# Front and middle of a hybrid state-space block: loads, weight buffers, product blocks, row copies and channel norm in another order

## The reference

```python
sh1, sc1, g1, sh2, sc2, g2 = split(silu(cond) @ ada_w + ada_b, 6)
h = rmsnorm(x + pos, norm1_g) * (1 + sc1) + sh1
z = h @ w_in                              # 1280 columns: 512 | 256 | 512
# 512: state-space mixer, 32 groups of 16 channels, 64 complex states, both directions
y = u * d + sum over directions of Re(C @ scan(lam_bar, B_bar @ u))
y = gelu(y); y_ssm = y * sigmoid(y @ w_glu + b_glu)
# 256: pooling, windows 2, 4, 8, 16: (mean - token) @ pool_w * scale
# 512: v = a * sigmoid(g); 31 depthwise taps; layer norm over 256 channels; silu
x = x + g1 * (concat(y_ssm, y_pool, y_conv) @ w_out)
h2 = rmsnorm(x, norm2_g) * (1 + sc2) + sh2
x = x + g2 * ((silu(h2 @ w1) * (h2 @ w3)) @ w2)   # then a last rmsnorm
```

## Time and profile before

| | us |
|---|---|
| three runs | 1328.51, 1330.0, 1331.0; median 1330.0 |
| profiled execution, first to last instruction (span) | 1323.8 |
| PE busy | 1220.8 (92%) |
| DVE, POOL, ACT busy | 850.8, 516.0, 511.0 |
| start of input projection block 0, end of block 29 | 66.8, 299.7 |
| glu tiles begin | 363.06 |

### The profile page before, as it was taken

How to read it: one execution, slowest core, us unless ns; L and a number is a source line. 1 busy time by engine, 2 the same in 40 slices (tenths; PEclk the granted TensorE clock), 3 DMA queues, 4 the chain that set the end, 5 groups by cost and what they waited for, 6 DMA issues and landing times.

```text
span 1323.8 us, 21436 instructions
## 1 busy us (share of the span) xinstructions
PE 1220.8 (92%) x7574; PEld 1080.5 (82%) x7574; DVE 850.8 (64%) x1338; ACT 511.0 (39%) x911; POOL 516.0 (39%) x360
## 2 busy tenths in 40 slices
PE   6786978995599999899999999999999999999996
PEld 4486877895545788799999999999889999999995
DVE  5538539959973427677666667766865555555558
ACT  2652531117235646633333333333532333334223
POOL 0595104376233101654444455444443233333340
PEclk9897988898799999999999999999999999999998
DMA  8815054389791331866665766666768777777771
GB/s 308 339 64 157 28 163 150 105 95 211 204 400 64 128 112 64 270 225 221 206 217 187 246 222 227 217 207 220 260 193 276 246 256 256 260 254 263 244 275 75
DMA packets 189570, 268.52 MB, mean 203 GB/s; under 512 B 14031, under 2 KB 108537, under 8 KB 186825
## 3 DMA queue, kind: packets, MB, share of 16 engines
q1 hardware_dynamic: 188144, 263.07, 60.6%
q0 software_dynamic: 1280, 4.72, 0.9%
q10 hardware_dynamic: 88, 0.02, 0.0%
HBM read 186.49 MB, written 81.26 MB: 202 GB/s over the span
## 4 chain that ended last, share of the span: by engine, by line
PE 76%; DMA 5%; issue 4%; POOL 4%; ACT 4%; DVE 3%; SPq 3%; DVEq 0%; ACTq 0%; POOLq 0%
PE banks L862 22%; PE banks L864 22%; PE banks L863 22%; PE banks L1131 3%; DMA ad<-in_ada_w 1%; PE banks L898 1%; PE banks L947 1%; SPq L436 1%; ACT nts L1660 1%; PE banks L1013 1%; POOL psum_w L751 1%; POOL sst L791 1%; DMA z_dram<-zp 1%; POOL pu L757 1%; PE banks L1136 1%
## 5 line engine op out<-in xcount | busy, mean ns | idle before, releaser
L814 POOL TENSOR_TENSOR raw13r<-raw13s,w13h 128x512 fp32r<-128x512 f32 x110 | 155.1, 1418 | 467.1 <-ACT w13h L1612 421.9
L863 PE MATMUL banks<-ntr,w13h 128*128 128x256 f32 (+1 forms) x1144 | 336.1, 294 | 0.0
L862 PE MATMUL banks<-ntr,w13h 128*128 128x256 f32 (+1 forms) x968 | 282.5, 292 | 4.4 <-ACT xs L1622 2.3
L863 PEld LDWEIGHTS banks<-ntr,w13h 128*128 128x128 f32 x1144 | 215.5, 188 | 0.9
L862 PEld LDWEIGHTS banks<-ntr,w13h 128*128 128x128 f32 x968 | 182.5, 189 | 6.5 <-ACT xs L1622 2.6
L862 PE MATMUL banks<-f2h,f_hi 128*128 128x512 f32 x396 | 156.6, 395 | 0.4 <-DVE acc L2317 0.4
L864 PE MATMUL banks<-f2h,f_lo 128*128 128x512 f32 x396 | 156.2, 395 | 0.0
L863 PE MATMUL banks<-f2l,f_hi 128*128 128x512 f32 x396 | 156.2, 394 | 0.0
L864 PE MATMUL banks<-ntr,raw13r 128*128 128x256 f32 (+1 forms) x528 | 153.5, 291 | 0.0
L2183 DVE TENSOR_TENSOR acc<-acc,banks 128x512 f32<-128x512 f32 x170 | 112.7, 684 | 38.9 <-PE banks L864 30.8
L818 POOL TENSOR_TENSOR f2l<-f2s,f2h 128x1024 fp32r<-128x1024 f32 x44 | 106.1, 2432 | 34.1 <-ACT f2h L1616 34.1
(11 more groups left out here) (323 smaller groups left out, 2536.4 us busy)
## 6 DMA issues: line engine op xcount, KB each, us to landing
raw13s<-in_ffn_w SPq DMA_DIRECT2D x66, 512.0 KB, 4.5
parts<-w13h SPq DMA_DIRECT2D x110, 256.0 KB, 2.4
w13h<-parts SPq DMA_DIRECT2D x110, 256.0 KB, 2.7
f2s<-in_ffn_w SPq DMA_DIRECT2D x44, 512.0 KB, 4.2
ad<-in_ada_w SPq DMA_DIRECT2D x20, 1024.0 KB, 9.8
parts<-wsumr SPq DMA_DIRECT2D x66, 256.0 KB, 2.6
wsumr<-parts SPq DMA_DIRECT2D x55, 256.0 KB, 4.9
parts<-raw13r SPq DMA_DIRECT2D x44, 256.0 KB, 2.9
```

The costliest lines, as they stand in the source:

```text
L814: nc.gpsimd.tensor_tensor(w13_low(x, f), w13_low(x, f, F32), w13h[x][:, :, :].bitcast(F32), ALU.subtract).then_inc(sem("w13_lo"), 1)
L862: nc.tensor.matmul(out, hi_w, hi_x, start=start, stop=False)
L863: nc.tensor.matmul(out, hi_w, lo_x, start=False, stop=False)
```

## The change

Front: on SP the first two `ada` pieces go ahead of `raws` and the position tables, x and columns of `w_in` follow in another order; four loads go to ACT's queue. A third buffer for `w_in` columns, low parts 0 and 1 on POOL and 2 on DVE. PE runs blocks 0 and 1 ahead of most turns, blocks 4 to 8 ahead of the first `wb_turn`, one block between the states' inputs, and in the loop two blocks for each two halves. Reading back `u` is split from writing `z`. DVE adds positions 4 to 7 later.

Middle: `sst` becomes four tiles; POOL copies all of quarter 0 right after the scan and half of each other quarter, ACT the other half between its evacuations of `y`; `u` has four buffers, and 2 and 3 are read between the `wc` quarters. Half of the last `y` writes go on ACT's queue. The gate of the first conv half moves up on POOL; the low parts of the glu product move from DVE to POOL. The channel mean comes after the last glu tile, the second mean after part of the output product.

```diff
-    wst = [at(f"wst{i}", [P, KT, P], O_WS + 4096 * i) for i in range(2)]
+    wst = [at(f"wst{i}", [P, KT, P], a) for i, a in enumerate((O_WS, O_WS + 4096, O_W2))]
-    sst = at("sst", [P, 2, Q, UC], O_NT + 36864)
+    sst = [at(f"sst{e}", [P, 2, 2, 4, UC], O_WB + 9408 if e == 0 else O_NT + 36864 + 9216 * e) for e in range(4)]
-    OUT = (4, 5, 0, 1, 6, 7, 2, 3)
+    OUT = (4, 5, 0, 1, 2, 3, 6, 7)
+    W_SLOT = (0, 1, 2, 0, 1, 0, 1, 0, 1, 0)
+    W_PRIOR = (None, None, None, 0, 1, 3, 4, 5, 6, 7)
+    LOW_POOL = (0, 1, 5, 6, 7, 8, 9)
+    def row_copy(e, r, d, par):
+        return (view(sst[e], (2 * par + d) * 4 * UC, [[UC, 4], [BL, NBL], [1, BL]], NS * r, NS),
+                view(st, r * Q * SLOTS + NPAIR * d + 4 * e, [[1, 4], [Q, NBL], [SLOT, BL]], NS * par, NS))
...
# SP: start
+        ada_in(0)
+        ada_in(1)
         for i, name in enumerate(("ssm_b_re", "ssm_b_im", "ssm_c_re", "ssm_c_im")):
...
-        for n in range(4):
-            x_in(n)
-            ada_in(n)
+        x_in(0)
+        ada_in(2)
+        x_in(1)
+        ada_in(3)
+        x_in(2)
+        x_in(3)
         ada_in(4)
...
+        for i in range(2):
+            z_saved(i)
+            sp.wait_ge(sem("z_out"), 16 * (i + 1))
+            u_first(i)
+        z_saved(2)
+        sp.wait_ge(*low_ready(3))
+        w_in_load(5)
+        z_saved(3)
+        sp.wait_ge(sem("z_out"), 64)
+        for i in range(2, 4):
+            sp.wait_ge(sem("v_done"), 8 * (i - 1))
+            u_first(i)
+        sp.wait_ge(*low_ready(4))
+        w_in_load(6)
...
+            if e in (1, 2):
+                u_again(e + 1)
...
# SP: y
-            if j + 2 < 4:
-                sp.wait_ge(sem("y_done"), 2 * (j + 1))
-                u_again(j + 2)
-            for t in range(CH):
+            for t in range(CH if j < 3 else CH // 2):
...
# POOL
+        w_low(0)
         pool.wait_ge(sem("gsc"), 1)
...
-        for n in range(8):
+        wc_piece(0)
+        w_low(1)
+        for n in range(1, 8):
             wc_piece(n)
+        w_low(5)
...
                     w_low(7 + 2 * j)
+                    if j == 1:
+                        gate_conv(0)
...
+        pool.wait_ge(sem("scan_done"), 1)
+        for r in range(2):
+            for d in range(2):
+                for par in range(2):
+                    nc.gpsimd.tensor_copy(*row_copy(0, r, d, par)).then_inc(sem("st_copied_pool"), 1)
+        pool.wait_ge(sem("st_copied_pool"), 8)
+        gate_conv(1)
...
         for m in range(4):
             glu_out(m)
             wo_low(m + 2)
+            y_low(m, ym[m % 2][:, :], m + 3)
...
# PE
         z_block(0)
-        x_turns(10, 13)
         z_block(1)
-        x_turns(13, 18)
+        x_turns(8, 18)
         z_block(2)
...
-        z_block(4)
-        z_block(5)
+        for s in range(4, 9):
+            z_block(s)
         wb_turn(0)
-        for s in range(6, 9):
-            z_block(s)
         wb_turn(1)
-        wb_turn(2)
         for s in range(9, 12):
             z_block(s)
+        wb_turn(2)
         wb_turn(3)
-        for j in range(4):
-            state_inputs(j)
+        state_inputs(0)
+        state_inputs(1)
         z_block(12)
+        state_inputs(2)
+        state_inputs(3)
+        z_block(13)
...
-        for m in range(8):
-            z_block(13 + m)
-            ade_half(m)
-            kb_half(m // 2, m % 2)
-        for s in range(21, 30):
+        for n in range(4):
+            z_block(14 + 2 * n)
+            ade_half(2 * n)
+            z_block(15 + 2 * n)
+            kb_half(n, 0)
+            ade_half(2 * n + 1)
+            kb_half(n, 1)
+        for s in range(22, 30):
             z_block(s)
...
         mod_turn(1, B[3])
+        glu_tile(2)
+        ada_tiles(2, 3, KT, B[4])
+        ada_bias_add(2, B[4])
+        glu_tile(3)
         pe.wait_ge(sem("tap_done"), 2 * TAPS)
         for b in range(NB):
             channel_mean(cacc, b)
-        glu_tile(2)
-        for b in range(NB):
-            pe.wait_ge(sem("dev_squared"), 2 * (b + 1))
-            channel_mean([lnw[:, 0, :], lnw[:, 1, :]], b)
-        ada_tiles(2, 3, 6, B[4])
-        glu_tile(3)
-        ada_tiles(2, 6, KT, B[4])
-        ada_bias_add(2, B[4])
...
         for c in (1, 2, 3):
             out_part(c, 0, 4, c == 1)
+        for b in range(NB):
+            pe.wait_ge(sem("dev_squared"), 2 * (b + 1))
+            channel_mean([lnw[:, 0, :], lnw[:, 1, :]], b)
         pe.wait_ge(sem("mod_evac"), 2)
         mod_turn(2, B[3])
         out_part(0, 0, 4)
+        for c in range(4):
+            out_part(c, 4, 6, c == 0)
         pe.wait_ge(sem("ln_root"), NB)
         pe.wait_ge(sem("mod_evac"), 3)
         gate_rows(1, 0, B[0:4])
-        for c in range(4):
-            out_part(c, 4, 6, c == 0)
```

More of the change, by code:

```diff
@@ L392, in _ @@
             ada_in(n)
+        x_in(4)
+        x_in(5)
         w_in_load(0)
-        for i in range(4, 8):
+        w_in_load(1)
+        for i in range(6, 9):
             x_in(i)
-        w_in_load(1)
-        x_in(8)
+        w_in_load(2)
         sp.dma_start(edge[:, :], A["pool_edges"]).then_inc(sem("edges_in"), 16)
@@ new lines, in z_saved, with u_first @@
+        def z_saved(i):
+            sp.wait_ge(sem("z_evac"), ZDONE[i])
+            sp.dma_start(dview(z_dram, i * P * CH * UC, [[CH * UC, P], [1, CH * UC]]),
+                         view(zp[i % 2], 0, [[1, CH * UC]])).then_inc(sem("z_out"), 16)
+        def u_first(i):
+            for s in range(CH):
+                sp.dma_start(u8[i % 2][16 * s:16 * s + 16, :, :],
+                             dview(z_dram, i * P * CH * UC + s * UC, [[CH * UC, 16], [16 * CH * UC, 8], [1, UC]])).then_inc(sem(f"u{i}_in"), 16)
@@ new lines, in _ @@
+        for i in range(2):
[13 more added lines that the diff above has]
+        for n in range(4):
+            if n == 0:
+                sp.wait_ge(sem("v_done"), 32)
+                ade_in(0)
+                ade_in(1)
+            else:
+                ade_in(2 * n)
+                ade_in(2 * n + 1)
+                kb_out(n - 1)
+            kb_weights(n)
+            if n >= 1:
+                sp.wait_ge(*low_ready(W_PRIOR[6 + n]))
+                w_in_load(6 + n)
+            if n == 0:
+                sp.wait_ge(sem("gaps"), 13)
+                for g in range(4):
+                    h = 64 * (g % 2)
+                    sp.dma_start(wpool[h:h + 64, g // 2, h:h + 64], dview(A["pool_w"], g * 4096, [[64, 64], [1, 64]])).then_inc(sem("wpool_in"), 16)
@@ L1395, in _ @@
             h_out(n)
-            if n >= 4:
-                square_sum(n)
+        w_high(1)
+        for i in range(4, 8):
+            square_sum(i)
         root(1)
-        w_high(1)
+        z_out(0)
         h_out(KT)
@@ L1402, in _ @@
         root(2)
-        for n in range(KT + 1, 13):
+        h_out(KT + 1)
+        z_out(1)
+        for n in range(KT + 2, 16):
             h_out(n)
-        z_out(0)
-        for n in range(13, 16):
-            h_out(n)
-        z_out(1)
+        w_high(2)
         h_out(16)
@@ L1465, in _ @@
             v_out(j)
-        w_high(5)
         z_out(12)
-        for m in range(8):
-            z_out(13 + m)
-            if m in (1, 4, 7):
-                w_high(6 + m // 3)
-            kb_evac(m // 2, m % 2)
-        for s in range(21, 30):
+        z_out(13)
+        for n in range(4):
+            z_out(14 + 2 * n)
+            if n in (0, 3):
+                w_high(6 if n == 0 else 8)
+            z_out(15 + 2 * n)
+            if n == 1:
+                w_high(7)
+            kb_evac(n, 0)
+            kb_evac(n, 1)
+        for s in range(22, 30):
             z_out(s)
@@ L1483, in state_copy @@
         def state_copy(e):
[L1484 to L1489 removed]
+            for d in range(2):
+                for par in range(2):
+                    A_(*row_copy(e, 1, d, par), ACT.Copy).then_inc(sem("st_copied_act"), 1)
         def y_out(c):
@@ L1511, in _ @@
         y_out(1)
+        state_copy(2)
+        y_out(2)
+        y_out(3)
         state_copy(3)
-        for c in range(2, 6):
+        for c in range(4, 8):
             y_out(c)
+        act.wait_ge(sem("y_evac"), 16)
+        for t in range(CH // 2, CH):
+            act.dma_start(dview(y_dram, 3 * P * CH * UC + t * UC, [[CH * UC, 16], [16 * CH * UC, 8], [1, UC]]),
+                          yb[1][16 * t:16 * t + 16, :, :]).then_inc(sem("y_out_act"), 16)
         wo_high(0)
-        y_out(6)
         wo_high(1)
-        y_out(7)
         act.wait_ge(sem("fin_turned"), 1)
@@ L1560, in _ @@
         y_high(1, ym[1][:, :])
+        glu_gate(2)
+        wo_high(4)
+        act.wait_ge(sem("scan_done"), 1)
+        mod_row_out(2, B[4])
+        act.wait_ge(sem("ada_tile"), 2 * KT + 4)
+        act.wait_ge(sem("glu_made"), 3)
+        y_high(2, ym[0][:, :])
+        glu_gate(3)
+        wo_high(5)
+        act.wait_ge(sem("glu_made"), 4)
+        y_high(3, ym[1][:, :])
         act.wait_ge(sem("ones"), 2)
```

204 lines of the change are left out of this document (80 added, 124 removed).

## The result

| | median us | runs | ratio to the kernel before, 95% interval |
|---|---|---|---|
| before | 1328.51 | 11 | |
| changed | 1321.55 | 11 | 0.9941 [0.9921, 0.9961] |

The change gains 0.6%, some 8 us (5 to 10.5), where 28.8 were forecast and the range went from 1289 to 1314. All runs here exceed their span by 1.8 us, so the execution profiled before took about 1325.6 by that; the 6.2 us that the forecast carried over held 4.4 us of run-to-run difference. That shifts the level, not the gain.

A forecast was written before the change was run, and what follows sets the result against it. PE was taken as the bound, busy 863.1 of 884.8 us, with 70 us idle before 439 to win. Gains of 31.6 and 2.8 less 5.6 lost in the tail made 28.8, so 1301.2 us, range 1289 to 1314.

The forecast's parts named there:

- the second: Rival: half stays, of `u` trips or `kbw` waits, or the front's 5.2 us in full; 1309 to 1315, chance .20.
- the fourth: Rival: nothing gained, early blocks only move the waits and the clock falls elsewhere; 1327 to 1333 us, chance .02.
- Z lies beyond 275: Sign of being wrong; Z is the end of the block loop's last block on PE, forecast at 268.1 us.
- The step that failed: Front, up to block 2: `pos_rows` about 3.4 us later, block 2 at 85.0, 0.7 later than before.
- The price by bytes for `ada`: Front: two 1 MB pieces ahead on SP, at 401 GB/s 2.6 us each, 5.2 us together.
- theory A: From the experiments, front: small loads' packets on ACT's queue take turns with SP's large ones, the last landing at 20.6 us.
- Block 2 to block 13: Input projection: 21.7 of 23.8 us idle go by the third buffer and covered `u` trips; block 13 ends at 172.2.
- rival 3: DVE becomes the bound, the taps end after 407 us; at 408 to 415 the time is 1331 to 1338, chance .03.
- The block loop: Block 13 to Z: `kbw` waits of 6.9 us hidden, 10.6 gained in all; bounds 6.9 and 13.3, or 3.
- Z to the glu tiles: First read of `y` at Z + 38.5, steps 8.0, 6.2, 4.3, PE on at Z + 60.5, 2.8 us earlier.
- The tail: From the glu tiles: 2.1 us lost at a modulation piece, 3.3 at the norm, 1.0 by collision, 0.8 gained; 5.6 lost.
- the 1.0: Tail: one collision of DVE's scaling with POOL's low parts in SBUF, 1.0 us taken between 0 and 2.4.

The follow-up runs named there:

- b_small_on_act: The kernel before with only the two states, the taps and d moved to ACT's queue: 1330.43 us, ratio 1.0027.
- b_ada_first: The kernel before with only the first two `ada` pieces put ahead of `raws` and the position tables on SP: 1332.32 us, ratio 1.0036.
- x5: The changed kernel with SP writing the second part of `y` before waiting for the first part's writes to land: 1312.75 us, ratio 0.9899.
- x3: The changed kernel with the four small loads back at SP's head and the first two `ada` pieces behind `raws` and position tables: 1308.62 us, ratio 0.9843.
- best1: The changed kernel with old load head, old channel norm place, early second `y` writes, and ACT's last kernel-half evacuation ahead of the gate's block: 1292.89 us, ratio 0.9738.
- best2: best1 with the second modulation's bias and the glu weight issued behind the first two parts of `y`: 1291.64 us, ratio 0.9749.
- x1: The changed kernel with the four small loads back on SP's queue, ahead of the first two `ada` pieces: 1315.65 us, ratio 0.9898.
- x2: The changed kernel with the first two `ada` pieces behind `raws` and position tables, small loads still on ACT's queue: 1311.02 us, ratio 0.9867.
- middle_only: The kernel before with only the middle's changes, the front as before: 1337.85 us, ratio 1.0065.
- x4: The changed kernel with the channel norm back between the glu tiles, low parts of `y` still on POOL: 1314.31 us, ratio 0.9882.

## Why the prediction was wrong

1321.55 us lies outside the forecast's range and in none of its rivals, between the 1315 of the second and the 1327 of the fourth. Its own sign of being wrong came: Z lies beyond 275.

**The step that failed** is the front's: "5.2 us, less some 1.8 of SP issues that go to ACT's queue". It booked the move of four small loads as 1.8 us of SP's time saved, and did not follow the loads themselves to their new queue, nor ask who waits for them. PE's first instruction waits for all of the small loads, 4.4 us longer with the move alone (b_small_on_act) and 13.8 with `ada` ahead. Nothing later has slack for that: position rows +10.4, and the front ends 15.8 us behind where 0.7 was forecast. The price by bytes for `ada` was right by itself: `pos_rows` landed 5.8 later in b_ada_first and 4.8 later in the changed kernel, against 5.2. So about 4.8 of the 10.4 are `ada`'s, and the rest is the wait for the small loads. With the head put back, 12.9 us return.

What a queue gets beside another one was not weighed. In the changed kernel ACT's queue got 12 packets beside 155 of SP's in 4 to 7 us, and 140 beside 235 in 7 to 12, and its last load landed at 20.6. The turns of theory A are a hypothesis: the runs show these counts and the landings, and not what decides which queue is served next.

The other part of the front, 3.4 us up to the turning of x, is the clock: 0.90 in 24.3 to 57.1, against 1.00 in 12 to 45.9 before. It isn't the price of the late start. In x5 PE began as late, at 20.58, and this stretch ran at 1.00 in 29.6 us; in x3 PE began at 6.16, and it ran at 0.93 in 32.0 (first position row to turning of x, x5 and x3):

```profile
24.21:53.80 29.59, 27.69 (x258) 14.20 (x256) 23.45 (x71) 11.41 (x21) 0.00 (x0) 1.00 0.79 294
13.83:45.84 32.01, 30.42 (x259) 14.21 (x257) 21.15 (x53) 9.48 (x17) 0.00 (x0) 0.93 1.03 394
```

What lowers the clock there in some executions is open. From the turning of x to block 2 it took 43.0 where 38.9 were forecast and 40.9 had been. The nine executions with the changed order of blocks range from 40.4 to 46.0, the four with the order of before from 40.9 to 48.3: a gain of the early blocks can't be seen there, and no row had shown that they would pay.

**Block 2 to block 13** held: 22.9 gained, 21.7 forecast. The third buffer does what it was priced for, the trips of `u` are covered. The scan began at 182.66 and ended 18.4 us ahead of Z; rival 3 (DVE as the bound) did not come, the taps ended at 360.3 and were wanted at 401.8.

**The block loop** gave 5.4 of 10.6. The `kbw` waits went, as forecast, but a new one came, and with it a slow stretch:

```profile
247.49 1.28 ACT L1437 ACT_TABLE_LOAD   x1 [8.24 <-PE banks L949]
...
249.17 0.57 ACT L1504 ACTIVATE kbp<-banks 32x512 f32<-32x512 f32 x1
```

ACT stood at the first gate column until PE had done the last piece of `ade` (L949), with the evacuation that PE waits for behind it. x3 and best1 differ in the loop by this order alone: from the end of block 13 to Z x3 took 101.0, best1 96.7, and best2 96.7 too (best1):

```profile
171.77:268.46 96.69, 96.69 (x641) 87.25 (x641) 94.47 (x131) 17.55 (x34) 62.13 (x44) 1.00 0.59 138
```

So with ACT's order mended the loop gave 9.8 of the 10.6, at a clock of 1.00. Of the 10.6 forecast, 3.7 were a share of the clock's loss beside the 6.9 of `kbw`, and 6.4 in the upper bound of 13.3; no run shows that share by itself. I had followed PE's order and SP's through the loop, and not ACT's.

**Z to the glu tiles.** The first read at Z + 36.9 against 38.5 is right; the steps from read to read were not: 9.3, 8.0 and 5.2 against 8.0, 6.2 and 4.3. They are a chain of waits on one queue; 6.2 is the lightest step of the kernel before, whose others were 12.6 and 7.0. (The forecast's own terms add up to Z + 60.7, not 60.5.)

**The tail**: both terms were right in kind, 2.4 for the modulation piece (2.1) and 3.8 for the low parts (3.3 and 1.0 together). Missing were 4.6 us more of busy time for the same 368 instructions (90.26 against 85.66): the clock was 0.91 instead of 0.98, and 0.51 behind the second of the two stalls. The other five executions with this tail (x1, x2, x3, x5, middle_only) took 94.8 to 96.5 us at 0.91 to 0.94. I priced stalls by their length alone. A stall doesn't always bring the lower clock: with the same two waits on POOL's output weight, 1.9 us in all, the tail ran at 0.93 in x4 and at 0.97 and 0.98 in best1 and best2; why is open. The two DVE scalings took 1733 and 1362 ns against 1372 before: 0.4, not the 1.0 taken for it. Only the first met POOL, for its first 0.5 us, and there POOL made the low part of an output weight, not of `y`. The 1.0 was an estimate of mine between 0 and the 2.4 of the earlier trace rows. The subtraction of 3033 ns there began at 535.03, beside one of POOL's from 534.13 to 537.52; that one collision costs the chain of the tail 1.0 no run shows.

## What to carry to other kernels

A load that is moved to another queue is a load with a new neighbour: find who waits for it, and what stands in front on the other queues, before its issue time is booked as saved. Give the smallest and first awaited loads the head of the first queue: with the old head of the loads 12.9 us came back. A chain of write, landing and read in one engine's order is cut by letting the next write go before the wait for the last (in x5 the second read came 6.8 us earlier), and a stall can cost more than its length: behind the second of two stalls of 1.9 us, PE ran at a clock of 0.51 for 4.1 us here.

## What the runs showed of the hardware that I had not expected

Two queues didn't share by bytes here: 90 KB on ACT's queue took until 20.6 us beside SP's, which moved some 5.7 MB by 21. In the stretch of the raws, which fill 32 partitions where `ada` fills 128, the DMA engines are as busy as elsewhere at half the rate: 184 to 213 GB/s at a share of 0.96 to 1.0 (7 to 12 us before, 12 to 16 with `ada` ahead), against 401 to 424 behind them. In x1 `pos_rows` landed 6 us later than bytes say, in b_ada_first and the changed kernel it did not; why is open. After the same late start the first 33 us of PE's work ran at a clock of 0.90 in the changed kernel and the first 30 at 1.00 in x5. The products right behind two stalls of 1.9 us, 1.3 us of work apart, ran at 0.51.
